# Four VectorE instructions of each GDN turn change their place in the order

## The reference, cut to what matters

```python
def gated_delta_rule(q, k, v, g, beta):      # chunks; L strictly lower triangular
    ...
    T = lax.linalg.triangular_solve(eye + L, ...)
    u = T @ vb
    w = T @ (kb * jnp.exp(g)[..., None])
    ...
    def step(state, inp):
        v_new = u_n - jnp.einsum('bhcd,bhde->bhce', w_n, state)
        o = q_n @ state + a_n @ v_new
        ...
def gdn_mixer(h, w_in, conv_w, A_log, dt_bias, norm_w, w_out):
    ...
    o = rmsnorm(o, norm_w) * silu(z)
    return o.reshape(B, S, GDN_V_WIDTH) @ w_out
```

## Time and profile before

| | before |
|---|---|
| median of 3 runs | 2736.06 us |
| the profiled execution | 2736.56 us |
| its span, first to last instruction | 2734.8 us |
| TensorE busy | 2681.2 us, 98% |
| VectorE busy | 1787.3 us, 65% |
| ScalarE busy | 1274.7 us, 47% |
| GpSimd busy | 899.6 us, 33% |
| mean granted clock of TensorE | 0.998 |

### The profile page before, as it was taken

The page is one execution under the profiler, slowest core; times in us unless marked ns, Lnnn a source line. Parts: engine busy times, 40 slices in busy tenths (PEclk is TensorE's granted clock), DMA queues, the critical chain, the costliest instruction groups (busy, mean ns, idle before and its releaser), DMA issues.

```text
span 2734.8 us, 40987 instructions
## 1 busy us (share of the span) xinstructions
PE 2681.2 (98%) x15550; PEld 2223.8 (81%) x15550; DVE 1787.3 (65%) x2641; ACT 1274.7 (47%) x2008; POOL 899.6 (33%) x751
## 2 busy tenths in 40 slices
PE   8999999999999999999999999999999999899998
PEld 6998888789888898887788998877777777777777
DVE  7974336569753687635956887348777777676664
ACT  4542232445323453223554543345555555467775
POOL 5520013136431264403733545104422222122232
PEclk9999999999999999999999999999999999999999
DMA  5343332223553325533213256322222222122222
GB/s 144 87 123 93 96 82 78 82 80 101 170 159 94 96 85 157 175 96 85 78 31 90 83 145 181 106 70 71 78 70 70 70 70 63 44 78 65 66 62 70
DMA packets 484876, 255.94 MB, mean 94 GB/s; under 512 B 17843, under 2 KB 478422, under 8 KB 484710
## 3 DMA queue, kind: packets, MB, share of 16 engines
q1 hardware_dynamic: 484534, 253.40, 32.4%
q10 hardware_dynamic: 176, 0.27, 0.0%
HBM read 251.51 MB, written 2.13 MB: 93 GB/s over the span
## 4 chain that ended last, share of the span: by engine, by line
PE 89%; DVE 6%; ACT 2%; issue 1%; POOL 1%; DMA 0%; SPq 0%; DVEq 0%; ACTq 0%; POOLq 0%
PE bank L281 60%; PE bank L978 12%; PE bank L2495 1%; PE bank L2526 1%; PE bank L2528 1%; DVE w_lo L267 1%; PE bank L2527 1%; DVE dsa_work L2191 1%; PE bank L3435 1%; PE bank L3427 1%; DVE small L2185 1%; PE bank L2640 1%; PE bank L3460 1%; DVE gdn_blocks L3030 1%; PE bank L1569 1%
## 5 line engine op out<-in xcount | busy, mean ns | idle before, releaser
L267 DVE TENSOR_TENSOR w_lo<-w_raw,w_hi 128x1024 fp32r<-128x1024 f32 x365 | 463.1, 1271 | 463.2 <-ACT w_hi L261 443.8
L281 PE MATMUL bank<-x_hi,w_hi 128*128 128x512 f32 x1808 | 737.7, 408 | 6.0 <-DVE w_lo L267 4.2
L281 PE MATMUL bank<-x_lo,w_hi 128*128 128x512 f32 x1808 | 707.8, 391 | 0.6 <-DVE x_lo L623 0.6
L281 PE MATMUL bank<-x_hi,w_lo 128*128 128x512 f32 x1808 | 707.5, 391 | 0.0
L261 ACT ACTIVATE w_hi<-w_raw 128x1024 fp32r<-128x1024 f32 x349 | 366.9, 1056 | 489.7 <-PE bank L281 440.7
L281 PEld LDWEIGHTS bank<-x_hi,w_hi 128*128 128x128 f32 x1808 | 340.4, 188 | 88.1 <-issue 16.5
L281 PEld LDWEIGHTS bank<-x_hi,w_lo 128*128 128x128 f32 x1808 | 340.1, 188 | 74.3
L281 PEld LDWEIGHTS bank<-x_lo,w_hi 128*128 128x128 f32 x1808 | 341.1, 189 | 68.1 <-DVE x_lo L623 3.9
L468 POOL TENSOR_TENSOR sumsq<-sumsq,sq 128x512 f32<-128x512 f32 x56 | 90.3, 1613 | 711.8 <-ACT sq L456 711.2
L281 PE MATMUL bank<-h_hi,w_hi 128*128 128x512 f32 x768 | 300.3, 391 | 0.0
L281 PE MATMUL bank<-h_hi,w_lo 128*128 128x512 f32 x768 | 299.0, 389 | 0.0
(11 more groups left out here) (542 smaller groups left out, 5070.1 us busy)
## 6 DMA issues: line engine op xcount, KB each, us to landing
w_raw<-in_ffn_wi_dram SPq DMA_DIRECT2D x176, 512.0 KB, 3.8
w_raw<-in_ffn_wo_dram SPq DMA_DIRECT2D x64, 512.0 KB, 3.5
w_raw<-in_ada_w_dram SPq DMA_DIRECT2D x48, 512.0 KB, 4.8
w_raw<-in_a_w_in_dram SPq DMA_DIRECT2D x48, 512.0 KB, 4.0
w_raw<-in_b_w_in_dram SPq DMA_DIRECT2D x32, 512.0 KB, 4.0
w_raw<-in_ffn_wo_dram SPq DMA_DIRECT2D x32, 384.0 KB, 3.1
w_raw<-in_even_w_in_dram SPq DMA_DIRECT2D x16, 512.0 KB, 4.0
w_raw<-in_a_w_out_dram SPq DMA_DIRECT2D x16, 512.0 KB, 3.5
```

The costliest lines, as they stand in the source:

```text
L267: dve.tensor_tensor(w_lo[s][:], w_raw[raw_of(b) % RAW][:], w_hi[s][:].bitcast(F32), ALU.subtract).then_inc(w_lo_done, 1)
L281: mm = pe.matmul(out, lhs[:, w], rhs(kt), start=first and kk == 0 and m == 0, stop=last and kk == len(kts) - 1 and m == 2)
```

## The change

In VectorE's list of each turn from 1 to 7, the two gated products go from ahead of the copies ga, gb to behind the sums ha, hb, and the two low halves of the output go from ahead of the sums va, vb (and the wait for product v) to behind them. Nothing else is changed: no instruction is added, removed or altered, and the lists of the other engines are the same.

```diff
                     conv(0, j + 1, i, at, odd)
-                if p is not None:
-                    gated(p, [gdn_gate(at, i, h)[3] for h in range(2)])
                 pe("g")
                 for n, r, src in (("ga", a, second(0)), ("gb", b, second(1))):
                     dve.tensor_copy(G.m[r, :], src[r]).then_inc(*done(n))
                 for n, r, src in (("ha", a, second(0)), ("hb", b, second(1))):
                     tt(n, halves(G.V1[r, :]), halves(src[r]), eye(r), ALU.add)
+                if p is not None:
+                    gated(p, [gdn_gate(at, i, h)[3] for h in range(2)])
                 pe("f2")
                 dve.tensor_copy(G.F2[b, :], first(1)[b]).then_inc(*done("f2b"))
                 splits("vc")
-                if p is not None:
-                    low(p)
                 pe("v")
                 own("hb")
                 for n, r, src in (("va", a, second(0)), ("vb", b, second(1))):
                     tt(n, G.V[r, :], G.V1[r, :], src[r], ALU.add)
+                if p is not None:
+                    low(p)
                 splits("f")
```

## The result

The changed kernel is slower: 2747.48 us median (2745.02 to 2748.23, 6 runs) against 2736.30 us (2734.93 to 2736.99, 6 runs), a ratio of 1.0039 with a 95% interval of 1.0027 to 1.0051, that is 11 us. The forecast was 2736.1 us, no change, with a range up to 2739.5.

What follows compares the result with a forecast made beforehand. TensorE, busy 98% of the span, was taken as the bound, so only its gaps count. Middle turns -4.5, last turn +3.1, clock +1.5 gave +0.1 us: 2736.1 us against a 2736.06 median, range 2733 to 2739.5.

Steps and rivals of the forecast that it cites:

- Copies first: Middle turns: ga, gb start in the gated products' slot, so f2 comes 1.20 us earlier and its gap is gone.
- What is late next: Middle turns: f2b ends 0.23 us later behind the gated products, so TensorE gets a new 0.8 us wait ahead of v.
- The dearer hand-overs: Middle turns: two more VectorE changes from upper to lower half make f2b later; without them 0.2 us better a turn.
- y comes 0.75 us earlier: Middle turns: 0.40 us kept from f2 plus y's closed 0.31 us gap, taken as 0.75; six turns win 4.5 us.
- The low halves run at once: Middle turns: low halves follow the sums without waiting, 2021.84 to 2023.13, and the split behind them ends at 2024.4.
- The rival in which the lead of the middle turns is not kept: Late Ob split holds TensorE behind y; six turns win nothing: +4.6 us, or +6.1 with second clock fall; chance 0.10.
- the cover: Middle turns: slack of 1.4 us between the end of the weight split behind the low halves and O0, its reader.
- The last turn: Turn 7: gated products delay f2b and v, low halves then delay O0; loss 3.1 us (2.8 to 3.4).
- The clock: Last turn: longer TensorE waits ahead of v and O0 likely lower the granted clock, costing 1.5 us.

Runs made afterwards that it cites:

- the filled last turn: Kernel before with the new order in the last turn alone, TensorE doing 8 and 10 unread matmuls in its waits ahead of v and O0: 2740.48 us.
- the last version: Kernel before, middle turns only: gated products behind f2b, low halves behind the sums, GpSimd released by k's first convolution instruction: 2727.45 us, ratio 0.9963.

## Why the prediction was wrong, step by step

- *Copies first: f2 comes 1.2 us earlier.* Right: the 1.2 us wait of the earlier trace rows is gone. In turn 1 0.38 us of its 1.6 stay.
- *What is late next: a wait of 0.8 us ahead of v, behind f2b.* Right: 0.74 us, f2b at 2016.60 where the forecast had 2018.42 less 1.82. The dearer hand-overs are in this number. The version with the gated products behind f2b shows that the wait was theirs: it disappears.
- *y comes 0.75 us earlier, six turns win 4.5 us.* Right for y and wrong for the turn. With GpSimd out of the way a middle turn of the new order takes 68.0 us, 0.7 less than before, in both versions that have the new order and the later release.
- *"The low halves run at once, 2021.84 to 2023.13", the split behind them ends at 2024.4.* This is the step that failed. The start was right to 0.02 us. Their durations I took from the earlier trace rows, where GpSimd stood still beside the low halves and started 0.05 us behind the split, so that the split kept its time. I had looked for waits that the moved instructions pass and found none of GpSimd's; I did not look for who waits for the instructions they are moved behind. vb releases GpSimd's stretch of 4.6 us. The move brought vb 2.1 us forward (from 2023.86 to 2019.99 + 1.82 = 2021.81) and put the two low halves ahead of the split there, so that three two-operand instructions stood behind vb and only the first had started before GpSimd. The split ended 2.06 us later than stacked, the convolutions with it; of these 2.06 us TensorE lost 1.65 a turn, 0.7 won became 0.95 lost.
- *The rival in which the lead of the middle turns is not kept* had the right sign and the wrong cause. It asked for a split that ends 1.4 us later than stacked, with the remark that nothing on VectorE there waits for anything but v. It ended 2.06 later without waiting, by lasting longer. O0 was not held by it: it starts 2.57 us behind y, as before (2.59), and only its fourth matmul, at 2024.69, reads the low half of Ob, 0.06 us after the split has ended. The forecast had taken the first matmul for the reader, so the cover was 0.7 us larger than its 1.4. TensorE was held further on, at O1, vn0 and ks1. The rival also had nothing won as its worst, and its highest price, with a second fall of the clock, was +6.1 us; the turns lost, and the whole came to +11.2.
- *The last turn: 3.1 us.* Right: 3.15 us with the clock held, in the trace of the filled last turn.
- *The clock: 1.5 us.* The fall was right, its size not: 2.6 us. I took the price from turn 0, where a fall lasts some 3.4 us; here there was little work between the two long waits and the low clock lasted from about 2362.9 to 2373.2. The forecast also took the kernel before as always at full clock in its last turn, from one trace; others show a fall there.
- The Trainium skill has the rule that I missed: the page GPSIMD Engine Reference, section "1. Specifications", states that the SBUF interfaces of GpSimd are shared with VectorE, with contention for VectorE instructions that have two SBUF inputs. The traces agree: the subtraction of two SBUF tiles went from 0.65 to 1.78 us beside GpSimd, the convolutions with one operand in PSUM did not change (2.31 us for three).

## What to carry to other kernels

Before moving an instruction, list who waits for the instructions that it changes places with, on engines with slack too, and see what their early start will run beside; a duration from the trace holds only with the same neighbours. Where VectorE's critical stretch has two-operand SBUF instructions, release GpSimd's slack work by a step behind which VectorE reads PSUM. A turn that has less filler than the others is to be stacked by itself, and given its own order.

## What the runs showed of the hardware

- The two engines did not slow down in proportion, they alternated by whole instructions: each one that found the other at work took 0.5 to 1.1 us longer, and the one that had started 0.05 us earlier kept its time (the split with 1.23 us beside GpSimd's 2.32). GpSimd's 128 x 512 sum takes 1.3 us where no such instruction of VectorE is beside it (2.55 us for two beside the convolutions), 1.8 and 2.3 behind one. This was looked at for VectorE instructions with two inputs in SBUF and for the convolutions with one in PSUM; no run here separates the count of the inputs from where they lie.
- The granted clock does not fall in every execution of the same instructions. With the last turn in its old order it stays at 1.00 in three traces (before, and the two versions with the new order in the middle turns alone) and falls to 0.50 for 6 to 7 us in three (the kernel before with the later and with the earlier release of GpSimd, and the last version). From 2360 to 2364, before and then with the later release:

```profile
2360.00:2364.00 4.00, 2.57 (x38) 2.09 (x38) 2.89 (x6) 2.60 (x5) 0.00 (x0) 1.00 0.00 0
2360.00:2364.00 4.00, 3.39 (x25) 2.60 (x21) 3.71 (x5) 1.62 (x3) 0.00 (x0) 0.50 0.00 0
```

  In the second the stretch from f2 to ks2 took 22.04 us instead of 19.9. With the whole new order in the last turn and no filler the clock fell in all three traces, for 10 us each. In turn 0, which the change does not touch, it fell in the traces of before and of all ten experiments and not in that of the changed kernel. That spares it 1.3 us (from product g to f2 2.67 us instead of 3.98), and is likely a part of why its profiled execution (2745.02) is the fastest of its six; the other five left no trace that would show it. A forecast of such a kernel to a microsecond or two is not to be had from one trace.
